# Logits of two banded attentions: fp32 products of depth 64 against pairs of float32r products of depth 128

## The reference, cut to what matters

```
def banded_attention(q, k, v, half_window, block, bias, sink):
    ...
    logits = jnp.einsum("bnqkgd,bnskd->bnkgqs", qb, kband).astype(jnp.float32) * scale + bias
    logits = jnp.where(mask[None, :, None, None], logits, NEG_INF)
    ...
    e = jnp.exp(logits - m)
    ...
    out = jnp.einsum("bnkgqs,bnskd->bnqkgd", p, vband)...

# C: three groups of four heads, (window, dilation) = (128, 1), (512, 4), (2048, 16)
# D: four query heads on two key heads, head width 64 everywhere
```

## Time and profile before

| | before |
|---|---|
| median of three runs | 3042.39 us |
| profiled execution, whole | 3043.13 us |
| its span, first to last instruction | 3041.1 us |
| mean granted TensorE clock | 0.978 |
| PE busy | 2854.2 us |
| DVE busy | 1218.3 us |
| ACT busy | 957.8 us |
| POOL busy | 625.7 us |

### The profile page before, as it was taken

How to read it: one execution, slowest core, us unless ns; L and a number is a source line. 1 busy time by engine, 2 the same in 40 slices (tenths; PEclk the granted TensorE clock), 3 DMA queues, 4 the chain that set the end, 5 groups by cost and what they waited for, 6 DMA issues and landing times.

```text
span 3041.1 us, 36561 instructions
## 1 busy us (share of the span) xinstructions
PE 2854.2 (94%) x13860; PEld 2235.8 (74%) x13860; DVE 1218.3 (40%) x2712; ACT 957.8 (31%) x2026; POOL 625.7 (21%) x337
## 2 busy tenths in 40 slices
PE   7899998899999989999979999988999999899997
PEld 5677886777777777777866778777877777677775
DVE  4474367521222245533145735574212223355222
ACT  3353115411332414411134621263023233244112
POOL 1200420032111131222230023201321112212322
PEclk9999999999999999999989999999999999999998
DMA  6100110021111221111130011100111113111122
GB/s 240 28 1 16 45 49 10 1 63 42 34 44 39 60 76 35 27 44 65 56 117 15 1 27 50 42 1 18 52 46 42 38 38 82 51 36 28 43 97 76
DMA packets 200966, 142.52 MB, mean 47 GB/s; under 512 B 20400, under 2 KB 185904, under 8 KB 200624
## 3 DMA queue, kind: packets, MB, share of 16 engines
q1 hardware_dynamic: 186960, 133.60, 15.5%
q10 hardware_dynamic: 13824, 6.49, 0.7%
HBM read 116.80 MB, written 23.27 MB: 46 GB/s over the span
## 4 chain that ended last, share of the span: by engine, by line
PE 84%; DVE 7%; ACT 4%; issue 2%; DMA 1%; POOL 1%; SPq 1%; POOLq 0%; DVEq 0%; ACTq 0%; another core or an unknown queue 0%
PE ps L858 21%; PE ps L821 8%; PE ps L823 8%; PE ps L822 8%; PE ps L959 8%; PE ps L969 5%; PE ps L984 5%; PE ps L917 4%; PE ps L918 3%; PE ps L919 3%; PE ps L1013 2%; PE ps L1014 2%; ACT yh L1454 2%; DVE yl L1769 2%; ACT prob L1298 1%
## 5 line engine op out<-in xcount | busy, mean ns | idle before, releaser
L1982 POOL CAST wh<-wraw 128x1024 fp32r<-128x1024 f32 (+2 forms) x162 | 177.0, 1092 | 2300.1 <-PE ps L823 924.8
L821 PE MATMUL ps<-xh,wh 128*128 128x512 f32 x1120 | 441.5, 394 | 3.0 <-ACT pt_split L1501 2.2
L822 PE MATMUL ps<-xl,wh 128*128 128x512 f32 x1120 | 437.7, 391 | 0.0
L823 PE MATMUL ps<-xh,wl 128*128 128x512 f32 x1120 | 437.7, 391 | 0.0
L1984 POOL TENSOR_TENSOR wl<-wraw,wh 128x1024 fp32r<-128x1024 f32 (+2 forms) x162 | 421.4, 2601 | 13.0
L858 PE MATMUL ps<-xh,wh 128*128 128x512 f32 x864 | 354.8, 411 | 1.2 <-ACT att L1320 1.2
L858 PE MATMUL ps<-xh,wl 128*128 128x512 f32 x864 | 345.2, 400 | 0.0
L858 PE MATMUL ps<-xl,wh 128*128 128x512 f32 x864 | 344.6, 399 | 0.0
L1626 DVE CUSTOM_DVE_ANT_0 prob<-ps,biasb 128x256 f32<-128x256 f32 (+3 forms) x192 | 78.1, 407 | 433.5 <-PE ps L959 433.2
L969 PE MATMUL ps<-ident,prob 128*128 128x128 f32 (+1 forms) x1520 | 235.0, 277 | 17.0 <-ACT prob L1298 16.8
L821 PEld LDWEIGHTS ps<-xh,wh 128*128 128x128 f32 x1120 | 211.9, 189 | 47.0 <-ACT pt_split L1501 3.0
(11 more groups left out here) (207 smaller groups left out, 4587.9 us busy)
## 6 DMA issues: line engine op xcount, KB each, us to landing
wraw<-in_w_in_dram SPq DMA_DIRECT2D x128, 512.0 KB, 3.9
xres<-acc SPq DMA_DIRECT2D x2, 4096.0 KB, 15.5
wraw<-in_w_branch_dram SPq DMA_DIRECT2D x64, 128.0 KB, 3.8
wraw<-in_w_out_dram SPq DMA_DIRECT2D x16, 512.0 KB, 3.8
acc<-xres SPq DMA_DIRECT2D x16, 512.0 KB, 6.9
dil_out<-cst ACTq DMA_DIRECT2D x96, 66.0 KB, 1.6
att<-dil_out SPq DMA_DIRECT2D x48, 132.0 KB, 2.5
acc<-in_x_dram SPq DMA_DIRECT2D x8, 512.0 KB, 8.9
```

What stands on the lines that cost most here:

```text
L821: pe.matmul(dst, ah, bh, start=i == 0, stop=False)
L822: pe.matmul(dst, ah, bl, start=False, stop=False)
L823: last = pe.matmul(dst, al, bh, start=False, stop=i == len(ks) - 1)
L1982: inc(pool.tensor_copy(high, raw), w_hi)
```

## The change

The logits of C and D become two float32r matmuls of depth 128 with the same stationary operand, as in branch B: a query head's high part in one half of the partitions and its remainder in the other, against the key's high part in both halves, then against its remainder in both halves. In C every product covers 256 columns, whatever the unit's band is; only the columns of the band are read afterwards (`seen`). The operands are made from the fill's PSUM bank: ACT writes the high parts (q: one copy of 64 partitions per head; k: two per head, the second into the other half), DVE subtracts them from the bank for the remainders (q one per head, k two per head). Two semaphores are new: `stack_twice`, after ACT's last copy of a k bank, and `stack_rest`, after DVE's last subtraction, which now frees the bank. In C the stacks lie over `yh` and `yl`, `gs`, `att` and `bk_stack`; D's values move to `rows_buf`, and `yn` and `b_last` change places there. D's projections are made in the order k, q, q, v instead of q, q, k, v, and its k banks are emptied between the two halves of the combination.

```diff
+        cq_stack = [yh[:, :, :], yl[:, :, :]]
+        ck_stack = [[gs_split[:, :, :], att_split[:, 0:2 * S].rearrange("p (f s) -> p f s", f=2)],
+                    [bk_stack[:, 0, :, :], bk_stack[:, 1, :, :]]]
...
-                                unit(cqT[hp][rows, i * P:(i + 1) * P], ckT[hp][rows, k0:k0 + nk],
+                                at = min(k0, S - 2 * P)
+                                unit(cq_stack[hp][:, e, i * P:(i + 1) * P], ck_stack[hp][e][:, 0, at:at + 2 * P],
                                      table_g[:, hp * 2 + e, b0:b0 + nk], chunks, "act",
-                                     st=i, head=hp * 2 + e, e=e, g=g, hp=hp)
+                                     st=i, head=hp * 2 + e, e=e, g=g, hp=hp, seen=(k0 - at, nk),
+                                     k_rest=ck_stack[hp][e][:, 1, at:at + 2 * P])
...
-                        unit(bqT[rows, h % 2, st * P:(st + 1) * P], bkT[rows, lo * P:hi * P],
+                        unit(bq_stack[:, h, st * P:(st + 1) * P], bk_stack[:, kv, 0, lo * P:hi * P],
...
-                             "dve", st=st, head=h, sink=True)
+                             "dve", st=st, head=h, sink=True, k_rest=bk_stack[:, kv, 1, lo * P:hi * P])
...
+                        elif kind == "v":
                             copies += 1
                             fill_freed_at.append((fill_freed, copies))
+                        else:
+                            rests += 1
+                            fill_freed_at.append((stack_rest, rests))
...
                 def wait_operands(p):
 
                     pe.wait_ge(t_freed_act, tgroups[p["v_groups"][-1][0]][1])
-                    pe.wait_ge(*fill_freed_at[p["fill_end"] - 1])
+                    pe.wait_ge(*fill_freed_at[p["fill"] + 5])
...
+                    place, seen = fill_tokens(p, half)
+                    for e in range(2):
+                        own = slice(e * HD, (e + 1) * HD)
+                        high = stack_at(p, kind, j, e)[0]
+                        inc(act.activation(place(high[own, :]), seen(bank[own, :]), ACT.Copy,
+                                           scale=-SCALE if kind == "q" else 1.0), stack_high)
+                    if kind == "k":
+                        for e in range(2):
+                            own, other = slice(e * HD, (e + 1) * HD), slice((1 - e) * HD, (2 - e) * HD)
+                            high = stack_at(p, kind, j, e)[0]
+                            ins = act.activation(place(high[other, :]), seen(bank[own, :]), ACT.Copy)
+                        inc(ins, stack_twice)
...
                             inc(act.activation(d_exp, d_arg, ACT.Exp), dil_exp)
+                            if half == 0:
+                                for j in range(2):
+                                    empty_fill(branches[3]["passes"][0], j, 3)
...
+                def stack_rests(p, f):
...
+                    if kind == "k":
+                        dve.wait_ge(stack_twice, twice)
+                    for e in range(2):
+                        own, other = slice(e * HD, (e + 1) * HD), slice((1 - e) * HD, (2 - e) * HD)
+                        high, rest = stack_at(p, kind, j, e)
+                        dve.wait_ge(stack_high, base + e + 1)
+                        if kind == "q":
+                            ins = dve.scalar_tensor_tensor(place(rest[other, :]), seen(bank[own, :]), -SCALE,
+                                                           place(high[own, :].bitcast(F32)), ALU.mult, ALU.subtract)
+                            continue
+                        for rows in (own, other):
+                            ins = dve.tensor_tensor(place(rest[rows, :]), seen(bank[own, :]),
+                                                    place(high[own, :].bitcast(F32)), ALU.subtract)
+                    inc(ins, stack_rest)
...
+                    if n == 2:
+                        for f in range(b["passes"][0]["fill"], b["passes"][0]["fill_end"]):
+                            stack_rests(b["passes"][0], f)
...
+                            k, i = divmod(s - u0, 16)
+                            if n == 2 and k + 1 < len(b["passes"]):
+                                after = b["passes"][k + 1]
+                                for j in range(2 * len(after["tiles"])):
+                                    if i == emptied_in(j):
+                                        stack_rests(after, after["fill"] + j)
...
+                            if half == 0:
+                                for f in range(windowed["fill"], windowed["fill"] + 2):
+                                    stack_rests(windowed, f)
                         for st in range(ST):
                             gated(b["y"][st], st)
+                        for f in range(windowed["fill"] + 2, windowed["fill"] + 6):
+                            stack_rests(windowed, f)
```

More of the change, by code:

```diff
@@ L184, in build @@
         araw = att[:, 4096 - ST * A_W:].rearrange("p (t c) -> p t c", t=ST)
[L185 to L190, removed]
+        bv = rows_buf[:, 2 * BW:2 * BW + S].rearrange("p (t c) -> p t c", t=ST)
         cv = [a.rearrange("p (t c) -> p t c", c=P) for a in (rows_buf[:, :], att[:, 2 * S:2 * S + 12 * P])]
@@ L325, in build @@
         stack_high = sem("stack_high")
+        stack_twice = sem("stack_twice")
+        stack_rest = sem("stack_rest")
         lg_ready = sem("lg_ready")
@@ L622, in build @@
         tile_used_at = {}
-        merges = toks = silus = copies = 0
+        merges = toks = silus = copies = rests = 0
+        fill_kind, fill_copy = [], []
         for b in branches:
@@ L659, in build, with stack_at, fill_tokens @@
                     tile_used_at[t] = (tok_ready, ST * (i + 1)) if i < 2 else (out_ready, ST * (i - 1))
+        STACKS_B = 2 * ST
+        def stack_at(p, kind, j, e):
+            if "g" in p:
+                if kind == "q":
+                    return cq_stack[p["hp"]][:, e, :], cq_stack[p["hp"]][:, e, :]
+                return ck_stack[p["hp"]][e][:, 0, :], ck_stack[p["hp"]][e][:, 1, :]
+            if kind == "q":
+                return bq_stack[:, 2 * e + j - 1, :], bq_stack[:, 2 * e + j - 1, :]
+            return bk_stack[:, e, 0, :], bk_stack[:, e, 1, :]
+        def fill_tokens(p, half):
+            if "g" not in p:
+                return lambda a: a[:, half * HALF:(half + 1) * HALF], lambda bank: bank
+            r = STRIDES[p["g"]]
+            w = HALF // r
+            return (lambda a: a.rearrange("p (c l) -> p l c", c=r)[:, half * w:(half + 1) * w, :],
+                    lambda bank: bank.rearrange("p (l c) -> p l c", c=r))
         DIL_PER_SLOT = len(branches[2]["passes"]) * 8 // 4
@@ L955, in logits @@
                     u = units[s]
-                    for c in range(0, u["nk"], HALF):
-                        w = min(HALF, u["nk"] - c)
+                    for c in range(0, u["k"].shape[1], HALF):
+                        w = min(HALF, u["k"].shape[1] - c)
                         rest = u.get("k_rest")
-                        ins = pe.matmul(u["logits"][:, c:c + w], u["q"], u["k"][:, c:c + w], start=True, stop=rest is None)
+                        dst = u["product_at"][:, c:c + w]
+                        ins = pe.matmul(dst, u["q"], u["k"][:, c:c + w], start=True, stop=rest is None)
                         if rest is not None:
-                            ins = pe.matmul(u["logits"][:, c:c + w], u["q"], rest[:, c:c + w], start=False, stop=True)
+                            ins = pe.matmul(dst, u["q"], rest[:, c:c + w], start=False, stop=True)
                     inc(ins, lg_ready)
@@ L1325, in empty_fill @@
                     j, half = divmod(j, 2)
-                    if n == 3:
-                        j = (j + 1) % 4
+                    kind = fill_kind[f]
                     act.wait_ge(fill_ready, f + 1)
                     bank = ps[:, fill_bank[f], :]
[L1330 to L1346, removed]
+                    if kind == "v":
+                        inc(act.activation(vT[:, half * HALF:(half + 1) * HALF], bank, ACT.Copy), fill_freed)
+                        return
+                    place, seen = fill_tokens(p, half)
[10 more added lines that the diff above has]
+                        inc(ins, stack_twice)
                 def empty_values(p, v, n):
@@ L1397, in _ @@
                         act.wait_ge(yn_set, 2)
-                        for j in range(6):
+                        for j in range(2, 6):
                             empty_fill(p, j, n)
@@ L1675, in silu @@
                                           ALU.mult), silu_done)
+                def stack_rests(p, f):
+                    j, half = divmod(f - p["fill"], 2)
+                    kind = fill_kind[f]
+                    if kind == "v":
+                        return
+                    _, count, twice = fill_copy[f]
+                    place, seen = fill_tokens(p, half)
+                    bank = ps[:, fill_bank[f], :]
+                    base = STACKS_B + 2 * (count - 1)
```

(6 more changed lines are left out.)

28 lines of the change are left out of this document (16 added, 12 removed).

## The result

The changed kernel takes 3066.39 us (median of 4 runs, 3063.27 to 3069.39) against 3042.33 us (3039.99 to 3043.92) before: a ratio of 1.0076, 95% interval 1.0063 to 1.0089, **slower by 0.76%**. The forecast was 3079 us, slower by 1.2%.

The account below looks back on a forecast made before the run. TensorE, busy 94% of the span, was taken to bound the kernel. 3043.1 - 82 (shorter logits) + 95 (waits for operands) + 24 (clock) = 3080 us, 3079 against the median; range 3037 to 3110.

Parts of the forecast that it names:

- The sign: Whole kernel: slower, 3079 us against the median, by 1.2%; slower by over 0.2% given chance 0.77.
- TensorE's gain: Logits products in C and D: 26.1 and 14.9 us a layer saved, 82 us in two layers.
- Making the operands, at the ends of passes: C's pass boundaries: TensorE waits for DVE's remainders, 7.6 us at each of four strided ends a layer, 3.7 at the contiguous.
- Before the first pass: Start of C: three more copies and four subtractions add 4.1 us to TensorE's 0.78 us wait, all lost.
- Rival 1: DVE's subtractions in C pay nothing for strided places: kernel at 3051 us, chance 0.22.
- Slot 14's stalls: C's passes 1 to 4: k's work in slot 12 delays transpose copies, 9.1 us a layer (low 1.9, high 17.1).
- The clock: After twelve new stops in C, TensorE resumes at clock 0.5: 2.0 us each, 24 us lost (low 0, high 29).
- Rival 2: At six resumptions a layer the clock isn't pulled down: 24 us go, 3027 with strides free too; chance of ending faster 0.14.
- What was to cost nothing: D's k and q operand making, hidden by the combination's load and fill matmuls; loads, rows_buf and moved yn: no cost.
- D's start: Eight k subtractions, 4.9 us, fit in DVE's 8.26 us idle during the combination's second load; no new wait.
- The sum: Whole kernel: 3043.1 - 82 + 95 + 24 = 3080 us, so 3079 against the median.

Follow-up runs that it names:

- experiment 6: Kernel before, fp32 logits of C and D over 128 rows, zeros in q's other 64 rows, k one plain copy; 2968.57 us, ratio 0.9755.
- experiment 9: Changed kernel, C's logits as one fp32r product of the head's own 64 high-part rows, remainders made but unused; 3095.19 us, ratio 1.0174.
- experiment 2: Changed kernel with C's fills written to contiguous places in all three patterns, tokens not reordered; 3013.9 us, ratio 0.9911.
- experiment 3: Changed kernel with 26 unread matmuls (16 at the contiguous boundary) before each wait between C's passes; 3049.54 us, ratio 1.0029.
- experiment 8: C exactly as in the kernel before, D as in the change; 3000.99 us, ratio 0.9859.
- 5's order: Changed kernel, next pass's first 24 fill matmuls before the boundary wait, C's banks filled v, k, q instead of v, q, k; 2992.64 us.

## Why the prediction was right, and where it was not

The sign, and the mechanism behind it, hold: more is lost at the ends of C's passes than the logits gain. By steps:

- **TensorE's gain: the step that failed.** I forecast 82 us; the runs show about 112 (C 70 instead of 52, D 42 instead of 30; D's own sum is 14.8 us a layer and not 14.9). I priced the product by its own line and wrote of the 0.1 us ahead of it that "this stays, since the next line (L984) is fp32". It went, and so did 0.1 us behind. What costs there is not a change of precision but of depth: 64-row weights among 128-row ones, 0.4 us a unit in fp32 (experiment 6) and in fp32r (experiment 9) alike. At depth 128 the fp32 product takes 0.43 us against 0.23 for the fp32r pair, so the precision is worth 0.2 at 256 keys; at 128 keys, where the pair still covers 256 columns, it is worth nothing (slots of 2.14 us in the change and 2.13 in experiment 6). The row was in front of me: 0.33 before L959 is a toll on entering, and a toll on entering suggests one on leaving. The Trainium skill (TensorEngine Tiling (Array Packing), Key Properties) states that changing the tiling mode drains TensorE. The traces agree as far as they go, with 0.1 us each way and another 0.2 in the product; that it is a drain and not only a weight load kept from running ahead, no run here tells. I had not weighed that rule.
- **Making the operands, at the ends of passes.** Forecast 7.6 us at each strided end and 3.7 at the contiguous one; layer 1 shows 6.97, 6.93, 7.35 and 7.56, and 4.55. Before the first pass 5.4 instead of 0.78, forecast 4.1 more, measured 4.7. DVE on strided places takes 1.03 us in a row (two in 2.05, above), forecast 1.05, against 0.69 for one contiguous. The Trainium skill (SBUF — State Buffer, the note on cachelines) states that an access which crosses to a new line pays a penalty; it gives no time, and the trace agrees: DVE stands with the strided ACT row. Rival 1, DVE free of it, is out; experiment 2 gives the strides' price, 52 us.
- **Slot 14's stalls.** 22.9 us more than before, forecast 18.2; in layer 1 3.06, 2.44, 2.44 and 3.42, forecast 2.25, 2.05, 2.05 and 2.75. In passes 1 and 4 the slots shrank more than I had thought, and TensorE asked 6.7 and 6.0 us into slot 12 instead of 7.1 and 6.6: the same error, seen from the other side. In passes 2 and 3 it asked at 7.3, as forecast. The rest is that the copies came at 9.8, 9.8, 9.8 and 9.5 instead of 9.35. (I had also taken pass 1 as 56.3 us long, where the earlier trace rows was cut; to the next pass's first logits it is 57.6. Slots 12 and 13 last 3.75 each all the same, as I had them.)
- **The clock.** Forecast 24 us for twelve stops; they cost about 27 (23 + 4, experiment 3), the whole about 37 by difference. I had left out that the stalls of slot 14 start the fall sooner, some 9 us: between 848 and 854 us, ahead of the long wait, the granted clock is 0.75 already. Rival 2, no clock loss, is out. That a gap in a loop is followed each time by a cold start, as the Trainium skill (TensorE: Matmul & The Clock Gate, HAM oscillation) has it, the trace bears out at all twelve stops: the granted clock in the slot behind them is 0.50 to 0.66.
- **What was to cost nothing.** D's start holds: the wait at L1074 is 17.1 us in all instead of 16.5, and experiment 8 puts D's part at a clear gain.
- **The sum.** 3042 - 112 + 98 + 37 = 3065 against 3043 - 82 + 95 + 24. A gain short by 30 us and a clock short by 13 partly cancel; that the forecast was nearer than its parts is luck.

What stays open: why the clock stayed up behind some of experiment 3's shortened stops and not behind others, and whether 5's order with more free banks would lose its new waits; no run combined them.

## What to carry to other kernels

Price a product by the whole stretch from the line before it to the line after it, and try the cheap half of a change alone: zeros in the unused rows gave 74 us here, with none of the operands that made the full change a loss. Work on DVE and ACT at the end of a pass needs TensorE work that doesn't depend on it issued in front of the wait; a low average share of those engines says nothing about it. Of a change over several stages, take each stage by itself: here one lost 65 us and the other gained 42.

## What the runs showed of the hardware

- A matmul with 64 rows of weights between ones with 128 costs about 0.4 us more than one with 128 rows and zeros in half of them: at 256 columns 0.10 on entering, 0.19 to 0.20 in it, 0.10 on leaving, in fp32 and fp32r; fp32 slots of 128 and 192 keys fell by 0.39 and 0.38 too. With another product of 64 rows behind it there is no such gain: in slot 3 of pass 0, 3.52 us with 64 rows and 3.68 with 128 in fp32, 3.27 and 3.46 in fp32r.
- Among products of 128 rows, one fp32r product of 64 rows and 256 columns takes 0.31 us, two of 128 rows 0.23 together.
- 512 fp32 elements into strided places: a DVE subtraction takes 1.01 to 1.08 us (0.68 to 0.70 contiguous), not far from ACT's copy with 1.09 (0.60).
- Idle matmuls that keep the clock up are worth their time only where they fit the wait: ten sets of them gave back 17.7 us and cost 4.0 where they overshot it or made its slot longer.
